# Attention scores as products over all 128 rows, with each head's queries copied by GpSimd into zeroed tiles

## What is computed

```python
# 6 heads "dil", 4 heads "dsa": head width 64
logits = jnp.einsum('bqhe,bqkhe->bqhk', qb, ksel) * (HEAD_DIM ** -0.5)      # + bias, masked
p = jax.nn.softmax(logits, axis=-1)
# 6 heads "mla": 64 columns without and 32 with rotary position, 96 in all
logits = (jnp.einsum('bqhe,bshe->bhqs', qn, k_nope) + jnp.einsum('bqhe,bse->bhqs', qr, k_r)) * scale
```

## Time and profile before

| | us |
|---|---|
| median of three runs (lowest to highest) | 2444.59 (2442.73 to 2445.73) |
| time of the profiled execution | 2440.64 |
| its span, first to last instruction | 2438.5 |
| TensorE, products, busy | 2185.7 |
| VectorE busy | 1610.5 |
| ScalarE busy | 1354.0 |
| GpSimd busy | 543.2 |

### The profile page before, as it was taken

The page is one execution under the profiler, slowest core; times in us unless marked ns, Lnnn a source line. Parts: engine busy times, 40 slices in busy tenths (PEclk is TensorE's granted clock), DMA queues, the critical chain, the costliest instruction groups (busy, mean ns, idle before and its releaser), DMA issues. The chain is left out here.

```text
span 2438.5 us, 31605 instructions
## 1 busy us (share of the span) xinstructions
PE 2185.7 (90%) x10840; PEld 1588.3 (65%) x10840; DVE 1610.5 (66%) x2260; ACT 1354.0 (56%) x1754; POOL 543.2 (22%) x310
## 2 busy tenths in 40 slices
PE   6999999799998998998679999997989899989956
PEld 5788756576676766665266886565766676766632
DVE  2583323588888877886545923246978788878847
ACT  3534631387777767676034355215867777767731
POOL 0001000242343333332000010003433333333310
PEclk9899999899999999999789999998999999999988
DMA  6213040699999999996721230408999999999965
GB/s 192 77 44 147 1 169 26 191 353 338 343 347 337 349 333 349 339 332 246 293 85 52 65 127 1 177 18 282 356 339 343 346 346 337 348 341 327 341 232 244
DMA packets 141434, 580.22 MB, mean 238 GB/s; under 512 B 40292, under 2 KB 65124, under 8 KB 88856
## 3 DMA queue, kind: packets, MB, share of 16 engines
q1 hardware_dynamic: 96280, 511.73, 58.3%
q0 software_dynamic: 45056, 67.22, 8.9%
HBM read 555.19 MB, written 61.37 MB: 253 GB/s over the span
## 5 line engine op out<-in xcount | busy, mean ns | idle before, releaser
L1193 POOL DMA_INDIRECT y_rows<-y,index x128 | 290.6, 2271 | 822.6 <-ACT y L1424 796.1
L1246 PE MATMUL ps_up<-w_hi,rowsT_hi 128*100 128x512 f32 x1024 | 422.0, 412 | 27.9 <-issue 19.0
L1248 PE MATMUL ps_up<-w_hi,rowsT_lo 128*100 128x512 f32 x1024 | 405.4, 396 | 0.0
L1390 ACT CAST w_hi<-w_other 128x2048 fp32r<-128x2048 f32 x128 | 245.7, 1920 | 184.7 <-DMA w_other<-exp_w 171.5
L1390 ACT CAST w_hi<-w 128x2048 fp32r<-128x2048 f32 x128 | 245.2, 1917 | 150.8 <-DMA w<-exp_w 87.0
L1327 DVE TENSOR_TENSOR w_lo<-w,w_hi 128x2048 fp32r<-128x2048 f32 x128 | 292.2, 2284 | 27.6 <-ACT w_hi L1390 27.5
L1327 DVE TENSOR_TENSOR w_other_lo<-w_other,w_hi 128x2048 fp32r<-128x2048 f32 x128 | 292.0, 2282 | 6.8 <-ACT w_hi L1390 6.7
L1271 PE MATMUL ps_y<-w_hi,hiddenT_hi 128*100 128x512 f32 x512 | 214.2, 418 | 74.3 <-issue 70.2
L1185 POOL DMA_INDIRECT rows<-x_rows,index x128 | 202.2, 1580 | 334.0 <-DVE index L1312 278.4
L1246 PEld LDWEIGHTS ps_up<-w_hi,rowsT_hi 128*100 128x100 f32 x1024 | 173.9, 170 | 86.0 <-issue 33.6
L1332 DVE TENSOR_TENSOR w_lo<-w,w_hi 128x2048 fp32r<-128x2048 f32 x96 | 219.1, 2283 | 2.7 <-ACT w_hi L1397 2.7
(11 more groups left out here) (228 smaller groups left out, 4135.6 us busy)
## 6 DMA issues: line engine op xcount, KB each, us to landing
w<-exp_w SPq DMA_DIRECT2D x232, 1024.0 KB, 15.1
w_other<-exp_w SPq DMA_DIRECT2D x128, 1024.0 KB
w_first<-exp_w SPq DMA_DIRECT2D x34, 1024.0 KB, 9.2
got<-y_rows SPq DMA_DIRECT2D x8, 4096.0 KB, 12.8
wbuf<-w_in SPq DMA_DIRECT2D x16, 1024.0 KB, 5.6
w_out_sb<-w_out SPq DMA_DIRECT2D x2, 4096.0 KB, 19.2
bias<-bias_tiles SPq DMA_DIRECT2D x2, 2560.0 KB, 9.0
sh_w<-sh_w SPq DMA_DIRECT2D x4, 1024.0 KB, 9.0
```

Of the source, the lines that this page charges most:

```text
L1193: pool.indirect_dma_start(d["y_rows"], bass.IndirectOffsetOnAxis(ap=index[0:CAP, x.step, 1:2], axis=0), y[0:CAP, x.slot, :], None, bounds_ ...
L1246: pe.matmul(ps_up[b][0:CAP], hi, w_hi, start=(k == 0), stop=False)
L1248: mm = pe.matmul(ps_up[b][0:CAP], lo, w_hi, start=False, stop=(k == KD - 1))
L1390: act.copy(w13_hi[:, :, k, :], w13[x.slot][:, :, k, :]).then_inc(S["up_hi_b" if half else "up_hi_a"], 1)
```

## The change

The scores of all heads are made over 128 rows. For the mla heads rows 96 to 127 of `mqT` and `mkT` are set to zero by GpSimd at the start of `_projections`. For the dil and dsa heads there is a new tile `q_pad` of four slots, zeroed once in each layer; GpSimd copies the 64 rows of a head's queries into a slot, at the same rows at which they lie in `dqkT` or `sqkT`, and the other 64 rows stay zero. The product then takes all 128 rows of the key tile, which hold the keys of two heads; those of the neighbour meet zeros. Slots are reused in turn, four heads later, so that the rows written in a slot are the same each time.

```diff
@@ _projections, GpSimd
+                for name in ("mqT", "mkT"):
+                    pool.memset(sb[name][MQ:P, :, :], 0.0).then_inc(S["rest_zero"], 1)
+                pool.wait_ge(S["rest_zero"], 2)
                 pool.wait_ge(S["unit_out"], place[("rest", 1, NT - 1)] + 1)
@@ _attention
+        q_pad = ctx.enter_context(nc.sbuf_tensor("q_pad", [P, PADS, SEQ], F32))
+        padded = [x for x in heads if x[0] != "mla"]
         def q_of(kind, h, i):
             cols = slice(i * P, (i + 1) * P)
-            a = HD * (h % 2)
-            if kind == "dil":
-                return sb["dqkT"][a:a + HD, h // 2, cols]
-            if kind == "dsa":
-                return sb["sqkT"][a:a + HD, h // 2, cols]
-            return sb["mqT"][0:MQ, h, cols]
+            if kind == "mla":
+                return sb["mqT"][:, h, cols]
+            return q_pad[:, padded.index((kind, h)) % PADS, cols]
+
+        def k_of(kind, h, w):
             if kind == "dil":
-                return sb["dqkT"][a:a + HD, H_DIL // 2 + h // 2, 0:w]
+                return sb["dqkT"][:, H_DIL // 2 + h // 2, 0:w]
             if kind == "dsa":
-                return sb["sqkT"][a:a + HD, H_DSA // 2 + h // 2, 0:w]
-            return sb["mkT"][0:MQ, h, 0:w]
+                return sb["sqkT"][:, H_DSA // 2 + h // 2, 0:w]
+            return sb["mkT"][:, h, 0:w]
@@ TensorE, scores(u)
+                    if kind != "mla" and i == 0:
+                        pe.wait_ge(S["q_padded"], padded.index((kind, h)) + 1)
@@ GpSimd
+                def pad(n):
+                    kind, h = padded[n]
+                    if n >= PADS:
+                        pe_done = NT * (heads.index(padded[n - PADS]) + 1)
+                        pool.wait_ge(S["scores_made"], pe_done)
+                    if n:
+                        pool.wait_ge(S["q_padded"], n)
+                    a = HD * (h % 2)
+                    src = sb["dqkT" if kind == "dil" else "sqkT"]
+                    pool.tensor_copy(q_pad[a:a + HD, n % PADS, :], src[a:a + HD, h // 2, :]).then_inc(S["q_padded"], 1)
+                pool.memset(q_pad[:], 0.0).then_inc(S["pad_zero"], 1)
+                pool.wait_ge(S["pad_zero"], 1)
+                for n in range(PADS):
+                    pad(n)
+                pool.wait_ge(S["q_padded"], PADS)
                 pool.wait_ge(S["bias_in"], 16)
...
+                pool.wait_ge(S["pen_added"], 3 * H_DSA)
+                for n in range(PADS, len(padded)):
+                    pad(n)
```

More of the change, by code:

```diff
@@ L296, in _projections @@
         S = _named(ctx, nc, "w_in w_hi w_lo xT_lo small_in unit_made unit_out rel_used "
-                            "squares mean_squares root latent_ready dve_step q_roped k_roped pool_step kr_zero")
+                            "squares mean_squares root latent_ready dve_step q_roped k_roped pool_step kr_zero rest_zero")
         wbuf = ctx.enter_context(nc.sbuf_tensor("wbuf", [P, KD, CHUNK_MAX], F32))
@@ L613, in _attention @@
     NS, NP, NTB = 3, 3, 2
+    PADS = 4
     with ExitStack() as ctx:
         S = _named(ctx, nc, "scores_made logits_out probs_out turned probsT_out heads_made head_out "
-                            "pen_added recips w_out_in bias_in")
+                            "pen_added recips w_out_in bias_in pad_zero q_padded")
         bias = ctx.enter_context(nc.sbuf_tensor("bias", [P, 10, SEQ], F32))
@@ L633, in q_of @@
             cols = slice(i * P, (i + 1) * P)
-            a = HD * (h % 2)
+            if kind == "mla":
+                return sb["mqT"][:, h, cols]
+            return q_pad[:, padded.index((kind, h)) % PADS, cols]
+        def k_of(kind, h, w):
             if kind == "dil":
-                return sb["dqkT"][a:a + HD, h // 2, cols]
+                return sb["dqkT"][:, H_DIL // 2 + h // 2, 0:w]
             if kind == "dsa":
-                return sb["sqkT"][a:a + HD, h // 2, cols]
-            return sb["mqT"][0:MQ, h, cols]
-        def k_of(kind, h, w):
-            a = HD * (h % 2)
-            if kind == "dil":
-                return sb["dqkT"][a:a + HD, H_DIL // 2 + h // 2, 0:w]
-            if kind == "dsa":
-                return sb["sqkT"][a:a + HD, H_DSA // 2 + h // 2, 0:w]
-            return sb["mkT"][0:MQ, h, 0:w]
+                return sb["sqkT"][:, H_DSA // 2 + h // 2, 0:w]
+            return sb["mkT"][:, h, 0:w]
         def v_of(kind, h, j):
```

## The result

The changed kernel takes 2414.86 us (median of six runs, 2409.82 to 2420.54), the kernel before 2442.52 in the same comparison (2434.52 to 2445.73). The ratio is 0.9896, with a 95% interval of 0.9879 to 0.9914: 21 to 30 us less, about 25. The profiled execution took 2420.54 us, 20.1 less than that of before.

What follows compares the result with a forecast made beforehand. TensorE, its products busy for 90% of the span, was taken to bound the kernel. Saving 11.4 us a layer, 22.8 for two, gave 2417.8 us profiled and, with 3.95 added for the runs' median, 2421.8; range 2412 to 2429.

Steps and rivals of the forecast that it cites:

- TensorE alone bounds these heads: In the dil and dsa heads, TensorE shows 66.00 of 66.00 us busy and nothing else holds them up.
- The dil and dsa heads take the mla pace: 5.50 us: Ten heads a layer take 55.0 us instead of 66.27, which saves 11.3 us a layer.
- The price is that of the passage between 64 and 128 rows, 0.29 us an S: In each 64-row unit, TensorE loses 0.29 us going from 128 rows to 64 and back (1.94 against 1.65).
- exposed loads: At S and T of 64-row heads, loads that were hidden start with, or 0.01 us before, their products.
- Another engine at the faster pace: In the sped-up heads, VectorE and ScalarE allow the pace of 5.50 us, and hardly more.
- the chain of 2.79 us: From S of unit 3 through VectorE and ScalarE to the same unit's T in an mla head: 2.79 us.
- GpSimd's copies and waits cost nothing: Copies into `q_pad`, memsets and waits on `q_padded` stay hidden: 0 us; bound for waits 2.4 us in all.
- The mla heads gain as well: Rival, 0.24: at S to T, 96 rows may cost 0.06 us; time 2414, or 2420 if the chain covers three of four.
- No change: Rival, 0.05: the slower pace has another cause than rows, such as queries and keys in one tile; 2444.6 us.
- slower: Rival, 0.05: loads over all 128 rows are exposed at S and T, costing 30 us; 2475 us.
- only part: Rival, 0.09: waits and uncovered copies give back 2.4 and up to 25 us for two layers; 2425 to 2437 us.
- the term of 0.13 behind the last S: After each layer's last S, T comes after 0.92 us instead of 1.05, another 0.13 us saved.

Runs made afterwards that it cites:

- the pairs order: Two S in a row at every second unit: in the kernel before 2432.13 us (0.9971), in the changed kernel 2428.48 us (0.9954).
- ahead3: The changed kernel with S issued three units ahead instead of two: 2413.39 us, ratio 0.9895 to the kernel before.
- copies64: The changed kernel with its memsets, copies and waits, but dil and dsa products over only the head's 64 rows: 2436.99 us, ratio 0.9994.
- mla96: The changed kernel with mla heads back at 96 rows and without the two projection memsets: 2413.48 us, ratio 0.9892.
- first64: The kernel before with mla head 0 alone over rows 0 to 63: 2440.81 to 2460.47 us in ten executions, ratio 1.0035.
- all64: The kernel before with all six mla heads over rows 0 to 63: 2453.45 us once, 2534.23 to 2535.95 three times.
- mla64: The changed kernel with mla heads over rows 0 to 63, without the projection memsets: four executions 2423.39 to 2431.03 us, six 2450.21 to 2461.67.
- rest64: The kernel before with mla heads 1 to 5 over rows 0 to 63, head 0 over 96: 2450.55 us, ratio 1.0041.

## Why the prediction was right, step by step

*TensorE alone bounds these heads.* Right. Every distance followed what TensorE's instructions did; only the pairs order made TensorE wait inside a head. One row of before seems to say otherwise, and the prediction passes over it: in the earlier trace rows the load of T is put down to ScalarE's `probs` (0.55). But ScalarE had finished these 128 columns two us earlier, at 281.43, and T starts at 283.51:

```profile
281.24 0.19 ACT L751 ACTIVATION_READ_ACCUMULATOR probs<-neg_logits,negmax 128x1 f32 x1
```

*The dil and dsa heads take the mla pace: 5.50 us.* Right: 5.49, 54.91 for ten heads where I had written 55.0. The 11.3 us of a layer are 11.36 in both layers.

*The price is that of the passage between 64 and 128 rows, 0.29 us an S.* Right, and shown from four sides: a quarter of the S gives 5.78, half the passages 6.11, all of them in another kind of head 6.64, all of them with the copies in place 6.64. That exposed loads are the mechanism is not shown as firmly: it rests on the timelines, where the loads move ahead of their products again, and no run separates the load from the passage. It may be that the passage stops TensorE and the load only stands behind it. The Trainium skill, page TensorEngine Tiling (Array Packing), section "Key Properties", says that a change of tiling mode drains the engine. The passages of 0.29 us agree with it.

*Another engine at the faster pace.* That none binds was right, the reason for the limit wrong. I argued that the chain of 2.79 us leaves hardly more than 5.50. ahead3 gave the chain more room and the pace stayed, so it is TensorE's own time.

*GpSimd's copies and waits cost nothing.* Right: the block of copies64 is that of before to 0.02 us. A copy takes 0.61 to 0.66 us, inside my bounds of 0.44 and 1.27; the memset of `q_pad` 1.81 against 1.76; the two others 2.65 against 2.6.

*The rivals.* "The mla heads gain as well" had 0.24 and falls: the mla heads take 5.49 us where they took 5.50, and S to T keeps its 0.91 to 0.92 us over 128 rows. The row that spoke for it is 128-row products in a long run; the 0.06 us that S has beyond them isn't due to 96 rows. What it is, no run tells. "No change" falls with copies64, "slower" with the loads that are ahead again, "only part" with 5.49 in every head. That rival was priced loosely: its own bounds of 2.4 and 25 us reach from 2424 to 2449, not to 2437, and the near half of 2425 to 2437 ends at 2431, not 2429. Nothing hangs on it, since the time fell on the other side.

*The sum.* The two blocks are 11.42 and 11.40 us shorter, 22.8 together, the very figure of the forecast. That it fits to a tenth is luck: the ten heads gave 11.36 a layer, not 11.27, and the term of 0.13 behind the last S hardly came. From that S to the first product behind the barrier it was 6.52 us and is 6.50, since the T of unit 3 waits there for ScalarE in both kernels; the forecast looked at the next T alone.

The profiled executions differ by 20.1: the blocks other than the attention took 2.7 us more in the one of after. Between the two attentions TensorE took 1097.9 to 1104.1 us in the profiles of all the kernels here, so one execution can't tell this from scatter. The runs, on the other hand, say 25 (21 to 30), and those of mla96 and ahead3 26. The 22.8 of the traces lies in all three intervals, and whether there are another 2 or 3 us, and where, stays open.

*The range.* Here was luck too. The forecast's own band was 2419 to 2425, and 2414.86 lies below it, in the part from 2412 on that the range had only for the rival "the mla heads gain as well". This rival is false. About 2 us of the distance come from the kernel before, which took 2442.52 in this comparison and 2444.59 in the runs on which the forecast stood; with its 22.8 that gives 2419.7. The other 5 are the size that I gave to what a measurement can tell. So the mechanism and its 22.8 us are shown by the blocks, and the median of the runs alone wouldn't have shown them.

## What to carry to other kernels

When products over 64 rows stand between products over 128 rows, count the passages: each, there and back, cost 0.29 us here. They vanish when the other rows are filled with zeros, and the filled rows cost TensorE no time (a head takes 5.49 us over 128 rows and 5.50 over 96). If filling needs copies, an idle engine and slots that are refilled some heads ahead hide them; 96 rows needed no filling. Before predicting, look for a part of the kernel that already does the work the other way: the mla heads gave the pace of the changed heads to 0.01 us.

## What I hadn't expected

TensorE's granted clock can depend on the rows of its products, or on what comes with them. Behind the barrier at the start of the attention, a head over 64 rows let it fall from the 2.4 to the 1.2 GHz level (first64, both layers; all64 and mla64, layer one). That didn't happen in every execution: by their times and mean clocks it did in three of four of all64 and in six of ten of mla64, and the two kernels kept the upper level in layer two of the same profiles. It stayed down as long as 64-row heads ran, with TensorE shown busy the whole time (180 of 180 us), at 12.19 us a head instead of 6.64. It came back only after some 3, 12 or 34 us of 96- or 128-row heads, and in all64 only in the next block.

With a head over 96 or 128 rows in first place it fell in no profiled attention, the ten 64-row heads of before and the fifteen of rest64 included. So the order of the heads protected the kernel before. The changed kernel has no 64-row head left that could start it; a padded head behind the barrier was not tried in another order. Whether the rows themselves matter or the passages beside them, no run separates, and why it fell in some executions only stays open. None of this was a term of my sum: the granted clock is 1.00 through the attention of both profiles, before and after.
